# Attention, gate product, combination of the groups and output product of one mixer as one part of the program

## What is computed

```python
def dilated_attention_mixer(h, w_in, w_out, rel_table):
    z = h @ w_in
    qkv = z[..., :B_QKV].reshape(bsz, s, B_N_GROUPS, 3, B_HEADS, B_HEAD_DIM)
    gate = z[..., B_QKV:]
    for gi, (window, dil) in enumerate(B_GROUPS):      # (128,1) (512,4) (2048,16)
        o, lse = dilated_window_group(...)
        outs.append(o); lses.append(lse)
    wts = jax.nn.softmax(jnp.stack(lses), axis=0)
    o = jnp.einsum('gbsh,gbshd->bshd', wts, jnp.stack(outs))
    y = o.reshape(bsz, s, B_WIDTH) * jax.nn.silu(gate)
    return y @ w_out
```

## Time and profile before

| | us |
|---|---|
| median of three executions | 3962.82 (3958.12 to 3965.83) |
| profiled execution | 3963.29, its span from first to last instruction 3961.2 |
| PE busy | 3656.8 (92% of the span) |
| DVE, ACT, POOL busy | 1872.1, 1215.6, 67.8 |
| granted TensorE clock, mean | 0.956 |

### The profile page before, as it was taken

One profiled execution on the slowest core, in us unless ns is written; L12 is line 12 of the kernel. 1 busy time (PEld: TensorE's weight loads), 2 busy tenths in 40 slices (PEclk: granted clock), 3 DMA queues, 4 the chain that ended last, 5 costly groups with the idle time before them and its releaser, 6 DMA issues. The chain is left out here.

```text
span 3961.2 us, 48530 instructions
## 1 busy us (share of the span) xinstructions
PE 3656.8 (92%) x18124; PEld 2947.4 (74%) x18124; DVE 1872.1 (47%) x3579; ACT 1215.6 (31%) x2326; POOL 67.8 (2%) x69
## 2 busy tenths in 40 slices
PE   8999999899999999999965879999935999999999
PEld 6888788777777777777754777777934778787887
DVE  4244244453334444444346254544577656654443
ACT  3233033233333333322312234444222432233222
POOL 0000100000000000000000000000010000000000
PEclk9999999999999999999977999999967999999999
DMA  4222143221111111112032120111221322232223
GB/s 139 97 84 69 62 124 110 72 70 53 45 47 54 50 50 51 48 44 60 18 120 106 60 89 23 46 41 61 83 96 56 98 96 82 77 108 92 97 96 120
DMA packets 155579, 296.60 MB, mean 75 GB/s; under 512 B 38912, under 2 KB 94256, under 8 KB 155168
## 3 DMA queue, kind: packets, MB, share of 16 engines
q1 hardware_dynamic: 142704, 265.54, 20.4%
q0 software_dynamic: 10608, 20.56, 1.6%
q10 hardware_dynamic: 2112, 8.39, 0.6%
HBM read 244.55 MB, written 56.11 MB: 76 GB/s over the span
## 5 line engine op out<-in xcount | busy, mean ns | idle before, releaser
L137 ACT ACTIVATE all_w_hi<-all_w_raw 128x1024 fp32r<-128x1024 f32 x303 | 318.3, 1051 | 587.3 <-PE om_z L152 261.4
L142 DVE TENSOR_TENSOR all_w_lo<-all_w_raw,all_w_hi 128x1024 fp32r<-128x1024 f32 x303 | 370.7, 1224 | 258.6 <-ACT all_w_hi L137 258.0
L902 PE MATMUL da_z<-all_hi,all_w_hi 128*128 128x512 f32 x736 | 305.8, 416 | 4.1 <-DVE all_w_lo L142 4.1
L902 PE MATMUL da_z<-all_hi,all_w_lo 128*128 128x512 f32 x736 | 291.1, 396 | 0.0
L902 PE MATMUL da_z<-all_lo,all_w_hi 128*128 128x512 f32 x736 | 289.6, 393 | 0.0
L858 ACT ACTIVATE at_p<-at_logit,da_pair_max 128x256 f32<-128x256 f32 (+1 forms) x384 | 177.9, 465 | 326.7 <-DVE da_pair_max L1058 325.8
L152 PE MATMUL om_z<-all_hi,all_w_hi 128*128 128x512 f32 x640 | 258.2, 403 | 7.6 <-DVE all_w_lo L142 4.5
L152 PE MATMUL om_z<-all_hi,all_w_lo 128*128 128x512 f32 x640 | 256.6, 401 | 0.0
L152 PE MATMUL om_z<-all_lo,all_w_hi 128*128 128x512 f32 x640 | 254.7, 398 | 0.0
L850 ACT ACTIVATE da_pt<-da_tr 128x512 f32<-128x512 f32 (+1 forms) x192 | 101.0, 526 | 477.1 <-PE da_tr L940 477.1
L152 PE MATMUL pr_g<-all_hi,all_w_hi 128*128 128x344 f32 (+1 forms) x624 | 213.8, 343 | 29.4 <-DVE all_lo L1922 24.8
(11 more groups left out here) (534 smaller groups left out, 7447.6 us busy)
## 6 DMA issues: line engine op xcount, KB each, us to landing
all_w_raw<-in_w_mlp SPq DMA_DIRECT2D x128, 512.0 KB, 3.3
all_w_raw<-in_w_ug SPq DMA_DIRECT2D x48, 512.0 KB, 4.2
all_w_raw<-in_w_qkv SPq DMA_DIRECT2D x48, 512.0 KB, 4.3
all_w_raw<-in_w_in SPq DMA_DIRECT2D x27, 512.0 KB, 3.4
da_w_raw<-in_w_qkv SPq DMA_DIRECT2D x24, 512.0 KB, 3.2
o_groups<-da_o SPq DMA_DIRECT2D x48, 256.0 KB, 2.9
bo_o<-o_groups SPq DMA_DIRECT2D x24, 512.0 KB, 5.2
all_w_raw<-in_w_v SPq DMA_DIRECT2D x20, 512.0 KB, 4.2
```

Of the source, the lines that this page charges most:

```text
L137: self.nc.scalar.activation(self.hi[b][:, :], self.raw[b][:, :], ACT.Copy).then_inc(self.hi_done[b], 1)
L142: self.nc.vector.tensor_tensor(self.lo[b][:, :], self.raw[b][:, :], self.hi[b][:, :].bitcast(F32), ALU.subtract).then_inc(self.lo_done[b], 1)
L902: last = nc.tensor.matmul(z[h][:, :], wp[u][:, ws], ap[:, kk, cols], start=(kk == 0 and m == 0), stop=(kk == KT - 1 and m == 2))
```

## The change

`attention_output` is gone; its work stands at the end of `dilated_attention`, without a barrier between. Call the weight units j: 0 to 7 gate, 8 to 15 output for tokens 0 to 511, 16 to 23 the same output weights again for tokens 512 to 1023 (each 24 products), 24 and 25 the next stage's first.

- Units 0, 1, 2 are multiplied inside turn 24, where the q, k, v products stood in the turns before. Units 3 to 7 follow.
- The log sums of the first two groups are stored in turn 24, those of the third after it, in 5 DMAs in place of 32.
- The combination of a token row m (128 tokens): group 0 is loaded into `all_yo` by POOL, groups 1 and 2 into four buffers `ol`. DVE scales group 0 (L1318 of the new file), POOL scales groups 1 and 2 (L892), DVE adds both (L1323).
- Transposes are spread over the units: a table `turned` says behind which unit PE transposes which groups. The gate is multiplied in place (`gated`), high parts by `upper`, low parts by `lower`.
- Units 8 and 9 are multiplied together, feature block by feature block, each as its low part is there.
- ACT copies the output products out and squares them straight from PSUM; the sum for tokens 0 to 511 is made behind unit 17.
- DMAs of constants moved from SP in `bo` to POOL at the start of `da`.

```diff
+        units = range(3, 24)
+        use = lambda j: (j % 2, turns + j // 2)
+        unit = lambda j: a_in["w_bo"][j] if j < 16 else a_in["w_bo"][j - 8] if j < 24 else a_in["w_in2"][(U_SQ, U_SK)[j - 24]]
+        gate_bank, out_bank, tr_bank = (z, pv), (z[0], z[1], pv[0], pv[1]), (tr[0], tr[1], qk[0], qk[1])
+        groups = [(m_, c) for c in range(2) for m_ in range(4)] + [(m_, c) for m_ in range(4, tiles) for c in range(2)]
+        turned = {5: (0,), 6: (1, 4), 7: (2, 5, 3, 6, 7), 9: (8, 9), 11: (10, 11), 12: (12, 13), 14: (14, 15)}
...
             schedule(sp, turn)
+            store_lse(2)
             sp.wait_ge(s_odma, 32 * turns)
+            for j in range(6, 26):
+                w.load(sp, *use(j), unit(j))
+                row = j - 4
+                if row < tiles:
+                    for g in (1, 2):
+                        n = 2 * row + g - 1
+                        sp.wait_ge(s_used, n - OL + 1)
+                        sp.dma_start(ol[n % OL][:, :], o_dram[g, row * P:row * P + P, :]).then_inc(s_ol[n % OL], 16)
+                if j == 19:
+                    sp.wait_ge(s_lo2, KT + tiles)
+                    sp.dma_start(x_again[:, :, :], x_out).then_inc(s_x, 16)
...
+        def _(pool):
+            pool.wait_ge(s_own, 1)
+            for m_ in range(tiles):
+                for g in (1, 2):
+                    n = 2 * m_ + g - 1
+                    part = by_head(ol[n % OL][:, :])
+                    pool.wait_ge(s_first[n] if n < OL else s_ol[n % OL], 16 * max(1, n // OL))
+                    nc.gpsimd.tensor_tensor(part, part, weight(m_, g), ALU.mult).then_inc(s_part, 1)
...
+                if j > 8 and j < 24:
+                    split(j + 1)
+                if j - 1 in turned and j > 8:
+                    for gi in turned[j - 1]:
+                        upper(gi)
+                h, c = out_of(j)
+                done(act, j)
+                nc.scalar.activation(yo[:, c, halves[h]], out_bank[j % 4][:, :], ACT.Copy).then_inc(s_ev, 1)
+                if c >= 2:
+                    act.wait_ge(s_yacc, 6 * h + max(1, c - 2))
+                elif h:
+                    act.wait_ge(s_ytot, h)
+                nc.scalar.activation(ysq[b], out_bank[j % 4][:, :], ACT.Square).then_inc(s_ysq, 1)
...
+            def transposes(gi):
+                m_, c = groups[gi]
+                pe.wait_ge(s_comb, m_ + 1)
+                wait(pe, s_y, gi - 3)
+                for k in range(4):
+                    last = nc.tensor.transpose(tr_bank[gi % 4][:, k * P:k * P + P], yo[:, m_, (4 * c + k) * P:(4 * c + k + 1) * P], ident)
+                last.then_inc(s_tr2, 1)
...
+            for j in range(3, 7):
+                done(dve, j)
+                for h in range(2):
+                    raw(j, h)
+                w.split_lo(dve, *use(j + 2))
+                finish(j)
+                if j == 3:
+                    weights()
+                else:
+                    combine(j - 4)
+                for gi in turned.get(j - 1, ()):
+                    gated(gi, slice(0, 4) if gi < 4 else slice(0, 3))
...
+                if j > 8:
+                    w.split_lo(dve, *use(j + 1))
+                if j - 1 in turned and j > 8:
+                    for gi in turned[j - 1]:
+                        gated(gi)
+                        lower(gi)
+                if (h, c) in ((0, 0), (0, 2), (0, 4), (0, 5)):
+                    combine(4 + {0: 0, 2: 1, 4: 2, 5: 3}[c])
```

More of the change, by code:

```diff
@@ L154, in products @@
         return last
+META = 16
+U_SQ, U_SK = 8, 10
 A_HEADS = 16
@@ L775, in turn @@
                         load_next(n + 1)
+                    elif n == turns - 1:
+                        for j in range(2):
+                            w.load(sp, *use(j), unit(j))
+                    else:
+                        for j in range(2, 6):
+                            w.load(sp, *use(j), unit(j))
+                        store_lse(0, 1)
                     sp.wait_ge(s_o, tiles * n)
@@ L836, in turn @@
                 a = n - 1
+                if isinstance(n, int) and n == turns - 1:
+                    act.wait_ge(s_exp, 2 * tiles * B_PAIRS)
+                    nc.scalar.activation(den[:, 0:2, :, :], den[:, 0:2, :, :], ACT.Ln).then_inc(s_ln, 1)
                 for s in range(SUB):
@@ L862, in _, with tanh, upper @@
             schedule(act, turn)
-            for b in range(2):
-                w.split_hi(act, b, turns, free=(s_piece[1], 3 * turns - 2 + b))
+            def tanh(j, cols=slice(0, T), n=0):
+                act.wait_ge(s_raw, 2 * j + 2 if n == 0 else 2 * j + n)
+                wait(act, s_gate, j - 1)
+                nc.scalar.activation(th[j % 2][:, cols], gate[:, j, cols], ACT.Tanh, scale=0.5).then_inc(s_th, 1)
+            def upper(n):
+                if n < KT:
+                    at = (slice(None), n, halves[0])
+                    act.wait_ge(*((s_y, 4) if n < 4 else (s_y7, 4) if n < 7 else (s_y, 8)))
+                else:
+                    m_, c = groups[n]
+                    at = (slice(None), slice(4 * c, 4 * c + 4), slice(m_ * P, m_ * P + P))
+                    act.wait_ge(s_y, n + 1)
+                nc.scalar.activation(hi[at], gate[at], ACT.Copy).then_inc(s_hi2, 1)
@@ new lines, in _ @@
+            dve.wait_ge(s_free, 1)
+            raw(7, 0)
+            combine(3)
+            done(dve, 7)
+            raw(7, 1)
+            w.split_lo(dve, *use(9))
+            for gi in turned[6]:
+                gated(gi, slice(0, 4) if gi < 4 else slice(0, 3))
+            finish(7, halves[0])
+            for gi in turned[7]:
+                gated(gi, slice(0, 4) if gi < 4 else slice(0, 3))
+            for n in range(4):
+                lower(n)
+            for gi in range(4, 8):
+                gated(gi, slice(3, 4))
@@ L1312, in attention_output @@
+            w.split_lo(dve, *use(25))
+    w.passed((turns + 12,) * 3, (10, 11, 0))
+    w.drop()
     return x_again
```

467 lines of the change are left out of this document (234 added, 233 removed).

## The result

The changed kernel takes 3904.7 us (median of 4 runs, 3899.0 to 3906.8) where the kernel before takes 3960.5 (4 runs on the same chip, 3955.5 to 3965.8): a ratio of 0.9857, with a 95% interval of 0.9839 to 0.9875, so 56 us or 1.4% faster. The prediction was 3907, with 3890 to 3930 as its range. The profiled execution took 3899.0 us, its span is 3897.3 us. How much of the 64 us between the two profiled executions is the change has to be read from the stages.

A forecast was written before the change was run, and what follows sets the result against it. PE and chains between engines bound it: after turn 24 ends at 2004.5, 170.0 us of work plus 38.7 of waits end at 2213.2, 56.2 us earlier, giving 3907 us (range 3890 to 3930).

The forecast's parts named there:

- The last turn: Turn 24, three gate units beside the attention: claimed 44.2 us store to store, ending at 2004.5.
- third rival: Turn 24's gate units only follow the attention: 57.1 us, not 44.2, so 13 us more, 3920; chance 0.05.
- The waits: PE idle between turn 24 and the last exponential: 38.7 us together, the largest 13.2 behind unit 6.
- fourth rival: POOL's dearer product slows row combinations: waits grow about 15 us per us; 3979 at 7 us; chance 0.03.
- Restarts: PE products at the slow clock after long waits behind turn 24: six, 5.8 us together (0 to 10.5).
- Transposes: PE's 64 transposes behind turn 24: 13.7 us, within 8.2 to 16.4.
- Shutting out: DVE and POOL products with both inputs in SBUF block each other: 9 us faster without it.
- first rival: DVE and POOL do not block each other: waits 32.0 us, 199.4 behind turn 24, kernel 3898; chance 0.18.
- Covers: Doubled weight loads, their high and low parts, POOL's twelve row loads and x's reload: hidden by PE's units, costed at nothing.
- The end: Last exponential of the stage: at 2213.2 against 2269.4 before, 56.2 us earlier.

## Why the prediction was right, point by point

- **The last turn.** 44.2 us predicted, 43.94 measured, and PE at 43.18 busy at the full clock. Putting the units behind the attention cost 14.0 us up to unit 3, against 13 in the third rival.
- **The waits.** 38.7 predicted behind the turn, 37.7 measured. Single ones: group 4 13.2 and 13.4; unit 12 6.5 and 6.5; unit 18 3.2 and 2.9; unit 16 1.0 and 1.0; unit 10 3.0 and 2.3; row 6 2.7 and 2.3. Their causes are shown by runs for group 4, for unit 18, and for unit 12 with row 6. Two places were off. For rows 0 and 1 the prediction had 3.6 and nothing, measured are 1.2 and 1.3 (its own figures for row 0, 14.3 less 11.1, give 3.2, not 3.6); POOL's product takes 1.90 us, not 2.3, which fits the smaller first wait. And from unit 7 to unit 8 it had 4.8 where there are 6.3 (4.36, 0.62, 1.34), since the low part of unit 9 ran into a POOL product and was held for 1.6 us; the prediction had let only `finish` be held there. That the total is so near is in part luck: these misses go both ways, each wait moves by up to about 1 us from one execution to the next, and by the prediction's own slope (fourth rival) POOL's 0.4 us less would have taken 6 us off the waits, where they came out 1.0 lower.
- **Restarts: too small.** The prediction had 5.8 us for products at the slow clock. Over the stretch's 620 products the distances between starts exceed 0.2316 us, the steady distance, by 9.7 us in all; in the other runs it was some 6.5 to 11. It said that a clock of 0.5 for more than the first 4 us behind a wait would prove it wrong in this, and behind the longest wait it was so:

```profile
2066.20:2070.20 4.00, 4.00 (x12) 3.32 (x13) 0.00 (x0) 0.00 (x0) 2.42 (x2) 0.50 0.89 304
2070.20:2072.20 2.00, 2.00 (x7) 1.57 (x6) 0.00 (x0) 0.00 (x0) 1.38 (x1) 0.53 0.03 10
2072.20:2080.48 8.28, 8.28 (x37) 6.67 (x36) 4.33 (x5) 0.63 (x1) 0.00 (x0) 1.00 0.14 38
```

- **Transposes: too large.** 13.7 predicted, 10.3 measured by the distances of their starts, since seven of the sixteen groups follow straight on a unit at the full clock. The two errors, +3.9 and -3.4, cancel; this part of the sum was right by luck: the total of 170.0 (measured 208.4 - 37.7 = 170.7) is nearer than its terms.
- **Shutting out.** It exists, on both engines, so the first rival (3898) falls. Its price was put at 9 us; POOL's products as a whole cost 7.4.
- **The fourth rival's slope.** "About 15 us for each us that it costs more" is not borne out: 1.9 us more per product, as a second instruction, cost 10.9, or 5.7 for each. The lists let POOL's whole price stand in DVE's way at once. One longer instruction of 3.8 us was not tried, so the slope for that form stays open. If the measured slope held further, an estimate, POOL's product would have to cost 56.9 / 5.7 = 10 us more before the gain is gone, and not the 6.0 us in all at which the prediction put the break-even.
- **Covers.** No wait on a weight stands before unit 20 or later, so x's load and the doubled weight loads were hidden as said. The twelve row loads were hidden too, but in an order that the prediction had not named: the log sums go first.
- **The end.** 2213.2 predicted, 2212.55 measured, in the profiled execution.

## What to carry to other kernels

Write out the engines' lists in their order with lengths from the rows, and follow PE through them: it gave the place of each large wait, and its size to within some 0.7 us (POOL's price and its consequences apart), where shares of busy time said nothing. A large wait at the head of an in-order list is often one short instruction behind long ones on another engine, and moving that one took 9.9 us off here for a wait of 13.4; look for what comes late next before you count it in full. Where two waits share a cause, as unit 12 and row 6, move the cause, not one of the loads. And before a small gain is put down to an edit, compare the granted clock at places that the edit does not touch: here 1.6 us came and went behind a wait of the same length.

## What the hardware showed that I had not expected

- DVE with two SBUF inputs and POOL's product alternate instruction by instruction: 2.92 us for 1.22 on DVE, 2.77 for 1.91 on POOL. It is what the Trainium skill says in "SBUF — State Buffer", section "Who interferes with whom" (an exclusive lock for the whole instruction), and here the trace agrees. The same section says that any GpSimd instruction that reads SBUF contends with such a DVE instruction; the run with one input doesn't agree in full: a DVE instruction ran at 1.22 us while POOL's ran, two others were held for 0.84 and 0.70 us, and the second ended while POOL's 2.77 us still ran.
- POOL's product of 1024 elements took 1.90 us, where the 3.99 us for 1792 elements in the earlier trace rows give 2.3. Half of it took 1.02. The multiplication by a constant, with one input less, took 2.77, so longer. By the rate in the Trainium skill, "GPSIMD Engine Reference", section "Elementwise — side-by-side cycle accounting", 1024 elements with two inputs would take 2.25 us, an estimate; the measurement is 0.35 less.
- How long the clock stays down behind a wait does not follow from the wait's length alone. Behind 2.89 us of idle PE before unit 18 the products that start from 2174.5 to 2177.4 lie 0.43 us apart in the changed kernel; behind the same 2.89 us in the run with SP's loads moved, and in the one with POOL's halves, none does. Behind the 2.3 us before unit 10 none was slow in the changed kernel; behind 2.2 us at the same place in the run with SP's loads moved seven were. In the changed kernel it stayed down for 6 us behind the 13.4 us, in the run with the earlier combinations for 3 us behind 14.0:

```profile
2068.19:2071.20 3.01, 3.01 (x9) 2.54 (x10) 0.00 (x0) 0.00 (x0) 1.78 (x1) 0.50 0.88 286
2071.20:2074.20 3.00, 3.00 (x14) 2.44 (x13) 0.00 (x0) 0.00 (x0) 2.03 (x2) 1.00 0.29 115
```

- Stores of 32 KB that took 2.4 us to land took 12.8 when 6 MB of another engine's loads were under way.
